# The attention mixers' output projection as products of 512 columns over both halves of the mixed value

## What is computed

```python
def _token_mixer(xn, w_in, w_pool, pool_scale, w_a, w_b, w_o, rel_bias):
    ...
    merged = jax.nn.sigmoid(g_pool) * (pool_out @ w_a) + jax.nn.sigmoid(g_attn) * (attn_out @ w_b)
    return merged @ w_o

def first_block(x, w_in, w_pool, pool_scale, w_a, w_b, w_o, norm1, norm2, ...):
    h = x
    for layer in range(DEPTH):                                   # DEPTH = 2
        h = h + _token_mixer(_rmsnorm(h, norm1[layer]), ...)
        h = h + _conv_ffn(_rmsnorm(h, norm2[layer]), w_up[layer], ...)
    return _rmsnorm(h, norm_f)
```

## Time and profile before

| | |
|---|---|
| median of 3 runs | 1520.1 us (1518.02 to 1520.16) |
| the profiled execution | 1518.61 us, its span 1516.8 us |
| PE busy | 1492.7 us, 98% of the span |
| DVE, ACT, POOL busy | 73%, 51%, 31% |
| mean granted TensorE clock | 0.997 of full speed |
| HBM | 177 GB/s over the span |

### The profile page before, as it was taken

How to read it: one execution, slowest core, us unless ns; L and a number is a source line. 1 busy time by engine, 2 the same in 40 slices (tenths; PEclk the granted TensorE clock), 3 DMA queues, 4 the chain that set the end, 5 groups by cost and what they waited for, 6 DMA issues and landing times.

```text
span 1516.8 us, 24876 instructions
## 1 busy us (share of the span) xinstructions
PE 1492.7 (98%) x10688; PEld 1361.0 (90%) x10688; DVE 1106.8 (73%) x1171; ACT 771.6 (51%) x872; POOL 474.9 (31%) x288
## 2 busy tenths in 40 slices
PE   8999999999999999999999999999999998999997
PEld 6899999988888999999888889989888897988886
DVE  6656666788777647666888666977887568788863
ACT  6433453666543334544666447356664444566642
POOL 2204400145698508000254733002443000134410
PEclk9999999999999999999999999999999999999999
DMA  7575444555556564366455444334555534355552
GB/s 255 183 234 181 139 158 177 190 178 188 181 189 257 193 231 158 137 232 250 170 192 195 153 170 151 137 115 167 193 178 179 199 118 140 125 181 195 181 187 76
DMA packets 48489, 269.72 MB, mean 178 GB/s; under 512 B 11483, under 2 KB 14811, under 8 KB 19452
## 3 DMA queue, kind: packets, MB, share of 16 engines
q1 hardware_dynamic: 48380, 268.13, 50.2%
HBM read 261.30 MB, written 6.82 MB: 177 GB/s over the span
## 4 chain that ended last, share of the span: by engine, by line
PE 93%; DVE 4%; DMA 1%; ACT 1%; issue 0%; SPq 0%; DVEq 0%; ACTq 0%
PE gemm L561 36%; PE gemm L590 33%; PE aux L590 16%; DVE w_lo L1420 1%; DMA raw<-in_weights 1%; PE aux L612 1%; PE aux L561 1%; PE gemm L671 1%; ACT w_hi L1048 1%; PE aux L788 0%; PE gemm L986 0%; PE gemm L673 0%; PE aux L648 0%; PE aux L661 0%; PE aux L684 0%
## 5 line engine op out<-in xcount | busy, mean ns | idle before, releaser
L1420 DVE TENSOR_TENSOR w_lo<-raw,w_hi 128x2048 fp32r<-128x2048 f32 (+3 forms) x246 | 575.3, 2342 | 188.2 <-ACT w_hi L1048 185.3
L1048 ACT ACTIVATE w_hi<-raw 128x2048 fp32r<-128x2048 f32 (+3 forms) x246 | 457.2, 1859 | 321.3 <-PE gemm L561 189.1
L561 PE MATMUL gemm<-x_two,w_hi 128*128 128x256 f32 x1952 | 355.1, 284 | 0.0
L561 PEld LDWEIGHTS gemm<-x_two,w_hi 128*128 128x128 f32 x1952 | 304.3, 192 | 0.7
L561 PE MATMUL gemm<-x_two,w_lo 128*128 128x256 f32 x976 | 276.1, 283 | 0.0
L590 PE MATMUL gemm<-x_two,w_hi 128*128 128x512 f32 x672 | 234.6, 399 | 0.0
L2121 POOL TENSOR_TENSOR tmp<-tmp 128x512 f32<-128x512 f32 x24 | 40.4, 1682 | 489.0 <-ACT tmp L1075 471.3
L561 PEld LDWEIGHTS gemm<-x_two,w_lo 128*128 128x128 f32 x976 | 187.0, 192 | 0.0
L590 PE MATMUL gemm<-y_two,w_hi 128*128 128x512 f32 x528 | 185.3, 396 | 0.0
L590 PE MATMUL gemm<-x_two,w_lo 128*128 128x256 f32 x672 | 174.9, 281 | 0.0
L2241 POOL TENSOR_TENSOR cv<-cv,rstd 128x512 f32<-128x512 f32 x44 | 116.2, 2641 | 182.2 <-ACT cv L1127 182.2
(11 more groups left out here) (373 smaller groups left out, 2741.9 us busy)
## 6 DMA issues: line engine op xcount, KB each, us to landing
raw<-in_weights SPq DMA_DIRECT2D x222, 1024.0 KB, 4.8
raw<-in_weights SPq DMA_DIRECT2D x16, 768.0 KB, 4.3
raw<-in_weights SPq DMA_DIRECT2D x8, 512.0 KB, 4.5
raw<-in_weights SPq DMA_DIRECT2D x4, 576.0 KB, 3.6
s_inputs<-s_made SPq DMA_DIRECT2D x1, 2048.0 KB, 10.1
s_outputs<-s_cw SPq DMA_DIRECT2D x1, 2048.0 KB, 12.1
s_v<-s_inputs SPq DMA_DIRECT2D x1, 2048.0 KB, 9.7
s_cw<-s_outputs SPq DMA_DIRECT2D x1, 2048.0 KB, 10.8
```

Of the source, the lines that this page charges most:

```text
L561: mm = pe.matmul(out, lhs, rhs, start=fresh and m == 0, stop=end and m == 2, skip_group_check=True)
L1048: me.give(act.activation(w_hi[i % SPL][:, 0:n], raw[i % RAW][:, 0:n], ACT.Copy), w_hi_ready)
L1420: me.give(v.tensor_tensor(w_lo[i % RAW][:, 0:n], raw[i % RAW][:, 0:n], w_hi[i % SPL][:, 0:n].bitcast(F32), ALU.subtract), w_lo_ready)
```

## The change

The four `wo` blocks of each of the two layers become `halves` blocks of two banks. `ph` and `pl` become two views of one tile `p_two`, high and low half of a chunk side by side, in the same 16 KB. PE runs `gemm_halves` for them. DVE adds the two halves to `h` in two instructions, the second waiting for the first (`me.settle()`), and `read_out` is signalled by the second.

```diff
-        plan += [Block("wo", layer, 256, DC, ftiles(256, DC), 1) for _ in range(4)]
+        plan += [Block("wo", layer, 256, DC, htiles(256, DC), 2, halves=True) for _ in range(4)]
...
-        ph = tile("ph", r_hid, [P, DC, S], F32R)
-        pl = tile("pl", r_hid + 8 * K, [P, DC, S], F32R)
+        p_two = tile("p_two", r_hid, [P, DC, 2, S], F32R)
+        ph, pl = p_two[:, :, 0, :], p_two[:, :, 1, :]
...
-                    gemm(first("wo", layer) + j, ph, pl, BY_PAIR if j == 0 else ())
+                    gemm_halves(first("wo", layer) + j, p_two, BY_PAIR if j == 0 else ())
...
                 if PLAN[i].halves:
                     first_half, second_half = halves_of(psum(i))
+                    if PLAN[i].kind == "wo":
+                        hh = hh.rearrange("p k (m c) -> p k m c", c=CLASS)
+                        first_half, second_half = (p.rearrange("p k (c m) -> p k m c", c=CLASS)
+                                                   for p in (first_half, second_half))
                     me.give(v.tensor_tensor(hh, hh, first_half, ALU.add))
                     me.settle()
                     me.give(v.tensor_tensor(hh, hh, second_half, ALU.add), read_out)
                 else:
-                    p = psum(i)
-                    if PLAN[i].kind == "wo":
-                        hh = hh.rearrange("p k (m c) -> p k m c", c=CLASS)
-                        p = p.rearrange("p (k c m) -> p k m c", k=2, c=CLASS)
-                    else:
-                        hh = hh.rearrange("p c s -> p (c s)")
-                    me.give(v.tensor_tensor(hh, hh, p, ALU.add), read_out)
+                    hh = hh.rearrange("p c s -> p (c s)")
+                    me.give(v.tensor_tensor(hh, hh, psum(i), ALU.add), read_out)
```

## The result

The changed kernel takes 1528.3 us (median of 6 runs, 1525.6 to 1529.5) against 1518.6 (6 runs, 1515.2 to 1520.2) of the kernel before, run beside it: a ratio of 1.0062, 95% interval 1.0051 to 1.0072, so 9.65 us slower. Predicted were 1526.3, range 1521.5 to 1529.5, from a loss of 7.0 us. The profiled execution took 1527.5 us, its span 1525.7, at a mean granted clock of 0.993 (before 0.997).

What follows compares the result with a forecast made beforehand. PE, busy 1492.7 of 1516.8 us, was taken as the bound. 1518.6 + 5.5 (stops less savings) + 1.5 (one clock fall) gave 1525.6, or 1527.1 against the runs' median; named 1526.3, range 1521.5 to 1529.5.

Steps and rivals of the forecast that it cites:

- the middle of two bases: Forecast time 1526.3 us, between 1525.6 from the profiled execution's 1518.6 and 1527.1 from the runs' median, 1.5 higher.
- The pair at 0.353: PE's 512 and 256 column products take 0.353 us against 0.360 for three of 256; a `wo` block takes 5.65.
- the 1.0 that the range allowed for it: Upper bound in us for DVE's second add, taken as 0.72, for a strided view and a busy PSUM.
- turn: Loop over DVE and ACT from one `wo` block's add to the next: grows from 6.19 to 6.91 us.
- The stop: PE stands still 3.2 us before chunk 6 in each layer's first `up_a` block, waiting for the last pair.
- T + 31.45: End of the first `up_a` block, counted in us from T, the first `wo` block's start; 28.70 before.
- The saving: Cheaper products in 8 `wo` blocks over two layers, all on PE's path: 0.9 us saved.
- the margin of 0.4: POOL's sum of the squares ends at T + 31.07, PE asks at 31.45; so it costs nothing.
- the rival of a delay taken back: PE's later waits after 990 us, 9.8 us in all, absorb the 5.5 delay; within no or short stall, 0.12.
- the other side: No stall, only the saving of 0.9 us: 1518.5 us; within no or short stall, chance 0.12.
- one fall in the two layers: +1.5: Clock drops to half speed behind one of PE's two new stops, 3.4 us at the lower level: 1.5 us.
- the rival with falls in both layers: Same stall, the clock falling behind both stops, 2 × 1.5 us: 1527.8 us; chance 0.27.

Runs made afterwards that it cites:

- one_add: The changed kernel without the second add behind the `wo` blocks, products and banks kept: 1518.0 us, ratio 0.9997 to the kernel before.
- two_adds_old_products: The kernel before with its old products, each `wo` block added to `h` twice by two DVE instructions: 1524.3 us, ratio 1.0044.
- w_hi_before_squares: The changed kernel with ACT making `w_hi` before the squares, not behind them, for the first three pairs: 1521.5 us, ratio 1.0017.
- dose_stop_2: The changed kernel, DVE making the second and third up blocks' `w_lo` after the last pair, whose low half is written two times more: 1523.4 us, ratio 1.0032.
- one-layer kernels: The change in layer 0 alone, and in layer 1 alone, the other layer keeping the old form: 1527.9 and 1528.3 us.

## Why the prediction was right, point by point

The measured 1528.3 lies in the range, 2.0 us over the number, on the side that was forecast. The loss missed by more: 7.0 us were forecast and 9.65 measured. The number started from the middle of two bases, about 1519.3, where the kernel before took 1518.6 beside the change, and these 0.7 us hid a part by luck.

**Prices and pace.** The pair at 0.353 held: a `wo` block is 5.67 in the chain (5.65). The spacing that the Trainium skill gives, page "TensorE: Matmul & The Clock Gate", section "Back-to-back issue gap", about 131 ns for 512 columns, does not hold here: 5.67 us for 16 pairs leaves no room for it, since the 256-column product alone takes 0.12 of 0.353 and leaves 0.233 for the other. The second add was 0.72 as taken from the earlier trace rows, also in the strided view, so the 1.0 that the range allowed for it, which no row backed, did not come; turn 6.92 (6.91 predicted).

**The stop.** The sum counted from start to start: 3.18 (3.2 predicted), `norm` at T + 31.49 (T + 31.45). The last pair came at T + 29.99 (30.04), and PE would have been at chunk 6 at T + 26.81 (26.84). `one_add` and `two_adds_old_products` show the second add to be its whole cause, and `w_hi_before_squares` that the loop runs over ACT as the sum had it. The saving is in the `wo` blocks, as small as said, but `one_add` shows that by itself it would hardly have reached the end: the pair was already as late as PE.

**The covers.** POOL's sum was in time, as its timeline shows, to compare with the earlier trace rows:

```profile
282.80 1.47 POOL L2120 TENSOR_TENSOR tmp<-tmp 128x512 f32<-128x512 f32 x1 [5.44 <-ACT tmp L1075]
```

It ended at 284.27, 0.41 before `norm`; the margin of 0.4 stayed. No later wait shrank, so the rival of a delay taken back fell, and so did the other side: the pair was in neither layer ready when PE wanted it. POOL's sum did not grow beside DVE either (1.47); where the two met in the kernels above, it was DVE's instruction that lasted longer, a price that the prediction does not have.

**The clock, the term that was mis-sized.** The step "about 1.1 to 1.7 us for a fall, I take one fall in the two layers: +1.5" priced every fall by one of 3.4 us at the lower level. (The same trace has a second, as long, at 42 to 47 us, which the prediction does not name.) In both of the change's profiles the fall in layer 1 lasted 6.8 us, and the first cost 2.8. The first profile itself is one fall at 2.8 instead of 1.5, and over the runs 2.3 to 3.9 us go with the clock instead of 1.5. This puts the measured time where I had the rival with falls in both layers (1527.8), but in neither profile did both layers fall; the runs without a profile don't say how many they had. The page of the Trainium skill named above, section "HAM oscillation — how this bites in real kernels", says that idle gaps between matmuls bring the gate back to half speed, but it speaks of longer gaps than these. The trace agrees in kind only: the fall in layer 1 came inside a stop of 3.0 us, and in `dose_stop_2` stops of 2.1 us had one. It is not certain for a given stop: of the change's four, two were without one.

**What stays open.** What decides whether a stop brings the clock down, and when: stops of 2.1 us had it twice in one profile, stops of 2.7 not at all in another. How many of the runs without a profile had a fall at a seam. And the "issue" stops of the one-layer kernels.

## What to carry to other kernels

Before adding 0.7 us to an engine at 73%, write down the loop in which that instruction stands and compare a turn with the time PE needs for one block: here 6.19 against 5.76 had already used up all slack, and nearly all of the four adds up to the last pair came through. A gain on PE is lost in the same place: with the loop as slow as before, cheaper products brought 0.1 us a layer. A long wait is ended by the last of a chain, so what is queued between two of its links is what to move: one `w_lo` of 2.2 us put behind the last pair took the whole loss back. Look also at what the moved instruction will then run beside: this one met POOL's sum and took 3.39 us. And price a stop of PE of 2 to 3 us at up to twice its length, as the granted clock may fall at it; one stop of 1.4 us had a fall that cost over three times as much.

## What was not expected of the hardware

At the same kind of stop the clock stayed down for 3.4 us in some profiles and 6.8 in others, and the longer case cost 2.8 us, almost as much as the stop itself. At the seams it was the longer wherever the clock was down before PE went on. The stops of 1.5 us at the seams (`w_hi_before_squares`) showed no fall, those of 2.1 did.

A DVE instruction that started while one of POOL's ran took 3.39 us instead of 2.29 (`w_lo`), or 1.39 instead of 0.48 (low half of a chunk).

Two kernels with 64 matmuls and their weight loads fewer ahead of the same place had stops of 1.4 and 0.7 us or a little more for which the profile shows no wait, and a fall at the longer (3.4 us in one, 10.2 in the other); before and the full change had none there. A kernel that changes half of something can thus cost as much as the whole for a reason of its own.
